# All later adaLN weight panels on VectorE, and one TensorE sum ahead of TensorE's third panel

## The chip, the core and the metric

The kernel runs on one core of one Trainium2 chip. The metric is the device time of one execution in microseconds. A core has TensorE (matrix products, PE in the profile; PEld are its weight loads), VectorE (DVE), ScalarE (ACT), GpSimd (POOL) and SyncE (SP, which here only issues transfers). Each engine runs its own queue in order; they wait for each other on semaphores.

## The reference, cut to what matters

The first of two blocks begins with an adaLN modulation: one vector `c` of 1024 is multiplied by a matrix of 1024 x 6144, and the six parts scale and shift what follows.

```python
mod = jax.nn.silu(c) @ w_ada[i] + b_ada[i]
shift_m, scale_m, gate_m, shift_f, scale_f, gate_f = jnp.split(mod, 6, axis=-1)

h = modulate(rms_norm(x, g_pre_mix[i]), shift_m, scale_m)
p = h @ w_in[i]
...
x = x + gate_m[:, None, :] * rms_norm(merged @ w_out[i], g_post_mix[i])
h = modulate(rms_norm(x, g_pre_ffn[i]), shift_f, scale_f)
...
x = x + gate_f[:, None, :] * rms_norm(f, g_post_ffn[i])
```

Only `shift_m` and `scale_m` (the first third of `mod`) are needed before the projection `h @ w_in`. The other two thirds are used later in the block. The sequence has 256 tokens.

## The kernel before, in words

**adaLN panels.** The matrix `w_ada` is cut into 24 panels of 128 x 2048 f32 (1 MB), each giving two columns of 128 of `mod`. Panels 0 to 7 are needed at once, before the projection. Panels 8 to 23 (the "later" ones, j = 0 to 15) are worked off between the panels of the projection. There are two ways to do a panel:

- On TensorE whole (`pe_ada_whole`, L824): 16 matmuls with the weights stationary and a moving operand of one column.
- On VectorE (`dve_ada`, L790 to L797): ten instructions multiply and add the panel's eight slices into a 128 x 256 sum in `sq_post`; then TensorE sums it over the partitions with two matmuls (`pe_ada`, L804). There are two such sums (`slot`), so VectorE's panel waits on `ada_done` until TensorE has summed VectorE's panel before last.

`ADA_TENSOR` names the panels that TensorE does whole: 1, 3, 5 and, of the later ones, 10, 14, 18 and 22. `ADA_ORDER` is the order in which TensorE comes to the panels: it sets the order of the first eight in its queue, and with `ada_summed` the value of `ada_done` for which others wait.

**Projection.** `h @ w_in` in this stage is 19 panels (`IN1_EARLY`) of 128 x 2048, each for 256 tokens. Weights are f32 and split into a high and a low part: when panel i is done on TensorE, ScalarE makes `w_hi` of panel i + 2 (L660, it reads `land`), then copies panel i's result out (L1373); VectorE makes `w_lo` of panel i + 2 (L667); TensorE then runs 48 matmuls on the panel (L696 to L698). There are two buffers. GpSimd takes each of the first ten results and does the token shift in three instructions (L1614 to L1619).

**Order on VectorE.** After `w_lo` of panel i + 2, VectorE does later adaLN panel j if `ADA_AFTER[j]` is i and the panel is VectorE's. `ADA_AFTER` is 0 to 7, 9 to 15 and 17, so that no adaLN panel stands behind i = 8, 16 and 18.

**Order on TensorE.** TensorE's part of later panel j stands behind projection panel `ADA_AFTER[j] + 2`, or + 1 for one that it does whole.

**SyncE.** It loads `w_in` panel by panel (waits for `lo_ready`), and ahead of some of them the adaLN panel j + 3, once the slot of panel j is free: for a panel of VectorE when its products are done, for one of TensorE when `ada_done` says so. All engines meet at the end of the stage (`stage_end`).

Of the kernel before, what the change touches and what calls it, by code (L numbers as in the profile page):

```python
# [53 lines left out]
ADA_FIRST, ADA_MORE = 8, 3  # L54
# [4 lines left out]
ADA_LATER = 24 - ADA_FIRST  # L59
# [2 lines left out]
IN1_EARLY = IN1 - IN1_ATT - IN1_LATE  # L62
ADA_AFTER = [i * (IN1_EARLY - 2) // (ADA_LATER - 1) for i in range(ADA_LATER)]
assert len(set(ADA_AFTER)) == ADA_LATER
ADA_TENSOR = (1, 3, 5) + tuple(ADA_FIRST + j for j in range(2, ADA_LATER, 4))
ADA_ORDER = (1, 0, 3, 2, 5, 4, 6, 7) + tuple(range(ADA_FIRST, 24))
ADA_VECTOR = tuple(sorted(set(ADA_ORDER) - set(ADA_TENSOR)))
ADA_VECTOR_FIRST = tuple(n for n in ADA_VECTOR if n < ADA_FIRST)
SINGLES, IN2 = 3, 19
# [514 lines left out]
def ada_summed(n):  # L584

    return ADA_ORDER.index(n) + 3

# [5 lines left out]
def load_with_ada(k, sp, d):  # L593

    for i in range(2, IN1):
        if i - 6 in ADA_AFTER:
            j = ADA_AFTER.index(i - 6)
            if j + ADA_MORE < ADA_LATER:
                n = ADA_FIRST + j
                if n in ADA_TENSOR:  # L600
                    sp.wait_ge(k.ada_done, ada_summed(n))
# [145 lines left out]
def pe_project(k, pe, start, count, tiles, W, loop=0, ready=None):  # L747

    n = W.stop - W.start

    def one(i, p, _):
        panel_begin(k, pe, p)
        for o in range(tiles):
            for t in range(KT):
                last = tile_mm(k, k.acc[:, 2 * p.par + o, 0:n], p.par, o * KT + t, k.h_hi[:, t, W],
                               k.h_lo[:, t, W], t == 0, t == KT - 1)
        last.then_inc(k.panel_done, 1)
    peeled = 0  # L760
    if ready is not None:
        p = Panel.of(start, loop)
        panel_begin(k, pe, p)
        for t in range(KT):
            pe.wait_ge(ready[0], ready[1] + (t + 1))
            for o in range(tiles):
                last = tile_mm(k, k.acc[:, 2 * p.par + o, 0:n], p.par, o * KT + t, k.h_hi[:, t, W],
                               k.h_lo[:, t, W], t == 0, t == KT - 1)
        last.then_inc(k.panel_done, 1)
        peeled = 1  # L770
    section(pe, start + peeled, count - peeled, one, loop)
# [45 lines left out]
def pe_ada_whole(k, pe, n):  # L817

    src = k.ada_first[:, n, :] if n < ADA_FIRST else ada_slot(k, n - ADA_FIRST)
    w = src.rearrange("p (o t c) -> p o t c", o=2, t=KT)  # L820
    ada_wait(k, pe, n)
    for o in range(2):
        for t in range(KT):
            last = k.nc.tensor.matmul(k.mb[:, 2, n * 2 + o:n * 2 + o + 1], w[:, o, t], k.csil_mean[:, t:t + 1],  # L824
                                      start=t == 0, stop=t == KT - 1)
    last.then_inc(k.ada_done, 1)
# [21 lines left out]
def pe_project_with_ada(k, pe):  # L848

    def column(n):  # L850
        if n in ADA_TENSOR:
            pe_ada_whole(k, pe, n)
        else:
            pe_ada(k, pe, n)
    pe_project(k, pe, 0, 1, 2, W1, ready=(k.hl_ready, 0))
    done = 0
    for i in range(1, IN1_EARLY):
        pe_project(k, pe, i, 1, 2, W1)
        while done < ADA_LATER and ADA_AFTER[done] + 2 - (ADA_FIRST + done in ADA_TENSOR) <= i:
            column(ADA_FIRST + done)  # L860
# [2057 lines left out]
def program_tensor(k, pe):  # L2918
# [6 lines left out]
    pe.wait_ge(k.csig, 2)  # L2925
    for n in ADA_ORDER[:ADA_FIRST]:
        if n in ADA_TENSOR:
            pe_ada_whole(k, pe, n)
# [300 lines left out]
```

## Time and profile before

| | |
|---|---|
| median of 3 runs | 2144.09 us (2142.82 to 2150.68) |
| the profiled execution's own time | 2144.94 us |
| its span | 2142.9 us |
| TensorE busy | 1988.7 us (93%) |
| VectorE busy | 1404.7 us (66%) |
| mean granted TensorE clock | 0.945 of full speed |

The span is from the first to the last instruction of the profiled execution; its own time is some 2 us more. The stage which the change touches is the first: it ends 197 us into the span. What stands behind it begins when all engines have met. A busy share over the whole span says little on a stage of 197 us, so the rows below are of that stage. A row of the timeline gives the start, the duration, the engine and line, what is written and read, and in brackets how long the engine had been idle and what released it.

### The profile page before, as it was taken

Reading aid. Unit: us, or ns where it says so; the run is one execution under the profiler, and the core shown is the slowest. Engines: PE = TensorE matmul, PEld = TensorE weight load, DVE = VectorE, ACT = ScalarE, POOL = GpSimd, SP = SyncE. Lnnn points to the kernel's source line nnn. Section 1 sums busy time; section 2 is a strip of 40 time slices with the busy share of each in tenths; the row PEclk is TensorE's granted clock in tenths of the full one; section 3 lists DMA queues with packets and bytes.
Section 4 is the critical chain, followed back from the end, with each engine's and each line's share of the span. In section 5 each row is a group of like instructions: output and inputs, shape, how many; then the busy total and the mean of one; then the engine's idle time right before and its main releaser. Section 6 shows DMA issues by size and latency. Waiting matters only on the chain.

```text
span 2142.9 us, 37023 instructions
## 1 busy us (share of the span) xinstructions
PE 1988.7 (93%) x14932; PEld 1909.4 (89%) x14932; DVE 1404.7 (66%) x2184; ACT 898.7 (42%) x1328; POOL 128.5 (6%) x182
## 2 busy tenths in 40 slices
PE   7898798996799999999999899999999999889997
PEld 6897688984699999998889889999999878889997
DVE  6865576765756557755755767756775565667774
ACT  3223254332455444443445454444444354444442
POOL 0520022200000000001100000000000200000000
PEclk7998798987899999999999999999999999999999
DMA  8565110002445535553323435543554322354552
GB/s 339 216 259 180 40 60 1 2 1 61 158 157 176 209 126 172 172 192 109 112 79 121 136 136 173 180 182 133 172 181 172 120 97 99 99 177 141 193 194 101
DMA packets 43447, 301.40 MB, mean 141 GB/s; under 512 B 4736, under 2 KB 6928, under 8 KB 11072
## 3 DMA queue, kind: packets, MB, share of 16 engines
q1 hardware_dynamic: 42736, 296.90, 39.8%
q0 software_dynamic: 592, 2.87, 0.4%
q8 instruction: 81, 1.33, 0.3%
q14 instruction: 38, 0.31, 0.0%
HBM read 298.70 MB, written 1.05 MB: 140 GB/s over the span
## 4 chain that ended last, share of the span: by engine, by line
PE 78%; DVE 10%; DVEq 4%; ACT 3%; issue 2%; DMA 2%; POOL 0%; ACTq 0%; POOLq 0%; SPq 0%
PE acc L696 20%; PE acc L698 20%; PE acc L697 20%; DVE w_lo L667 2%; ACT w_hi L660 2%; PE mb L824 2%; PE acc L2559 2%; PE mb L719 1%; PE mb L1967 1%; PE acc L1967 1%; DVEq L1403 1%; PE mb L2531 1%; DMA land<-in_w_out 1%; PE mb L1964 1%; DVE gla_sq L2897 1%
## 5 line engine op out<-in xcount | busy, mean ns | idle before, releaser
L696 PE MATMUL acc<-h_hi,w_hi 128*128 128x272 f32 (+1 forms) x2960 | 875.6, 296 | 45.4 <-DVE w_lo L667 19.5
L697 PE MATMUL acc<-h_lo,w_hi 128*128 128x272 f32 (+1 forms) x2960 | 858.2, 290 | 0.0
L698 PE MATMUL acc<-h_hi,w_lo 128*128 128x272 f32 (+1 forms) x2960 | 856.3, 289 | 0.0
L667 DVE TENSOR_TENSOR w_lo<-land,w_hi 128x2048 fp32r<-128x2048 f32 (+2 forms) x251 | 576.9, 2299 | 203.0 <-ACT w_hi L660 202.7
L660 ACT ACTIVATE w_hi<-land 128x2048 fp32r<-128x2048 f32 (+2 forms) x251 | 481.8, 1920 | 523.0 <-PE acc L698 461.6
L696 PEld LDWEIGHTS acc<-h_hi,w_hi 128*128 128x128 f32 x2960 | 571.8, 193 | 59.1 <-DVE w_lo L667 21.7
L697 PEld LDWEIGHTS acc<-h_lo,w_hi 128*128 128x128 f32 x2960 | 573.2, 194 | 2.0 <-issue 0.2
L698 PEld LDWEIGHTS acc<-h_hi,w_lo 128*128 128x128 f32 x2960 | 573.9, 194 | 0.0
L696 PE MATMUL acc<-a_hi,w_hi 128*128 128x272 f32 (+1 forms) x880 | 252.3, 287 | 0.6 <-DVE w_lo L667 0.3
L698 PE MATMUL acc<-a_hi,w_lo 128*128 128x272 f32 (+1 forms) x880 | 252.4, 287 | 0.0
L697 PE MATMUL acc<-a_lo,w_hi 128*128 128x272 f32 (+1 forms) x880 | 251.4, 286 | 0.0
L696 PEld LDWEIGHTS acc<-a_hi,w_hi 128*128 128x128 f32 x880 | 166.1, 189 | 1.3 <-DVE w_lo L667 0.9
L697 PEld LDWEIGHTS acc<-a_lo,w_hi 128*128 128x128 f32 x880 | 165.9, 188 | 0.0
L698 PEld LDWEIGHTS acc<-a_hi,w_lo 128*128 128x128 f32 x880 | 165.5, 188 | 0.0
L1094 ACT ACTIVATE sq_post<-acc 128x272 f32<-128x272 f32 (+1 forms) x48 | 18.0, 392 | 184.4 <-PE acc L698 184.4
L1250 DVE TENSOR_TENSOR t_ff<-acc,ssum 128x272 f32<-128x272 f32 (+1 forms) x88 | 38.5, 437 | 83.5 <-PE acc L698 81.1
L696 PE MATMUL acc<-y_hi,w_hi 128*128 128x256 f32 (+1 forms) x192 | 57.3, 298 | 17.8 <-DVEq L546 13.6
L1119 DVE TENSOR_SCALAR f<-acc,vec 128x272 f32<-128x272 f32 (+1 forms) x40 | 19.9, 497 | 74.5 <-ACT sq_post L1094 73.9
L2468 POOL MEMSET sel<- 40x1024 f32 x2 | 1.9, 942 | 1045.8 <-PE acc L707 1045.8
L2336 DVE TENSOR_TENSOR p<-acc,ssum 128x272 f32<-128x272 f32 (+1 forms) x56 | 24.2, 432 | 49.3 <-PE acc L698 48.9
L696 PEld LDWEIGHTS acc<-y_hi,w_hi 128*128 128x128 f32 x192 | 37.2, 194 | 21.3 <-issue 19.2
L697 PE MATMUL acc<-y_lo,w_hi 128*128 128x256 f32 (+1 forms) x192 | 55.3, 288 | 0.0
(519 smaller groups left out, 2589.7 us busy)
## 6 DMA issues: line engine op xcount, KB each, us to landing
land<-in_w_gu SPq DMA_DIRECT2D x110, 1024.0 KB, 4.9
land<-in_w_in SPq DMA_DIRECT2D x65, 1024.0 KB, 4.9
land<-in_w_down SPq DMA_DIRECT2D x40, 1408.0 KB, 6.0
ada_first<-in_w_ada SPq DMA_DIRECT2D x24, 1024.0 KB, 8.6
land<-in_w_ab SPq DMA_DIRECT2D x24, 512.0 KB, 3.5
land<-in_w_out SPq DMA_DIRECT2D x12, 1024.0 KB, 4.9
land<-in_w_in_single SPq DMA_DIRECT2D x6, 512.0 KB, 3.5
const<-in_const POOLq DMA_DIRECT2D x1, 1134.0 KB, 7.9
```

Source lines behind the costliest of these rows:

```text
L660: k.nc.scalar.activation(k.w_hi[:, p.par, 0:size * P], k.land[:, p.par, 0:size * P], ACT.Copy).then_inc(k.hi_ready, 1)
L667: k.nc.vector.tensor_tensor(k.w_lo[:, p.par, 0:size * P], k.land[:, p.par, 0:size * P], k.w_hi[:, p.par, 0:size * P].bitcast(F32), ALU.sub ...
L696: mm(out, k.w_hi[:, par, c], hi, start=start, stop=False)
L697: mm(out, k.w_hi[:, par, c], lo, start=False, stop=False)
L698: return mm(out, k.w_lo[:, par, c], hi, start=False, stop=stop)
L719: r = k.nc.tensor.matmul(k.mb[:, 2, 0:n], k.mean_ones[:, :], moving, start=done == 0, stop=done == KT)
L824: last = k.nc.tensor.matmul(k.mb[:, 2, n * 2 + o:n * 2 + o + 1], w[:, o, t], k.csil_mean[:, t:t + 1], start=t == 0, stop=t == KT - 1)
L1250: v.tensor_tensor(k.t_ff[:, t % 2, W], k.acc[:, 2 * p.par, 0:n], c, ALU.mult).then_inc(k.t1_ready, 1)
L1403: dve.drain()
L1967: last = mm(bank[:, 1, c * P + lo:c * P + hi], m["x_bd"][:, c, :], m["xr"][:, c, lo:hi], start=True, stop=True)
L2336: k.nc.vector.tensor_tensor(chunk_tile(k, l, c), k.acc[:, 2 + o, 0:W.stop - W.start], k.scale[:, W], ALU.mult).then_inc((k.chunk_free, k.a ...
L2559: last = mm(k.acc[:, 0, lo:hi], k.fvz[0:chi - clo, i % 2, c, h, :], k.fpt[0:chi - clo, h, c, 0:n], start=(h == 0 and c == 0), stop=(h == 1 ...
```

## The change

Panels 10, 14, 18 and 22 leave `ADA_TENSOR`, so VectorE does all sixteen later panels. In `ADA_ORDER` panels 4 and 5 change places. SyncE's order stays; four of its waits turn from `ada_done` to `ada_products`.

```diff
-ADA_TENSOR = (1, 3, 5) + tuple(ADA_FIRST + j for j in range(2, ADA_LATER, 4))
-ADA_ORDER = (1, 0, 3, 2, 5, 4, 6, 7) + tuple(range(ADA_FIRST, 24))
+ADA_TENSOR = (1, 3, 5)
+ADA_ORDER = (1, 0, 3, 2, 4, 5, 6, 7) + tuple(range(ADA_FIRST, 24))
```

On TensorE, ahead of the projection (`mb` holds the sums, `sq_post` is what VectorE made, `ada_first` the panels as they landed):

```order
 L804 MATMUL mb<-mean_ones,sq_post 128x1 [waits ada_products]
 L804 MATMUL mb<-mean_ones,sq_post 128x1
+L804 MATMUL mb<-mean_ones,sq_post 128x1 [waits ada_products]
+L804 MATMUL mb<-mean_ones,sq_post 128x1
 L824 MATMUL mb<-csil_mean,ada_first 128x1 [waits ada_first_landed5]
 L824 MATMUL mb<-csil_mean,ada_first 128x1 x15
```

The first pair is the sum of panel 2; the pair with + is the sum of panel 4, which stood behind panel 5's sixteen matmuls and now stands ahead of them.

On TensorE behind projection panel 3, before:

```order
L804 MATMUL mb<-mean_ones,sq_post 128x1 [waits ada_products]
L804 MATMUL mb<-mean_ones,sq_post 128x1
L824 MATMUL mb<-csil_mean,ada_first 128x1 [waits ada_first_landed10]
L824 MATMUL mb<-csil_mean,ada_first 128x1 x15
L696 MATMUL acc<-h_hi,w_hi 128x256 [waits acc_free,lo_ready]
```

The same place with the change:

```order
L804 MATMUL mb<-mean_ones,sq_post 128x1 [waits ada_products]
L804 MATMUL mb<-mean_ones,sq_post 128x1
L696 MATMUL acc<-h_hi,w_hi 128x256 [waits acc_free,lo_ready]
L697 MATMUL acc<-h_lo,w_hi 128x256
L698 MATMUL acc<-h_hi,w_lo 128x256
```

Panel 10's sixteen matmuls are gone from between the two projection panels; a pair like the first stands behind the next projection panel instead. It is so at three more places.

On VectorE, between `w_lo` of projection panel 4 and of panel 5:

```order
-L667 TENSOR_TENSOR w_lo<-land,w_hi 128x2048 [waits hi_ready] x2
+L667 TENSOR_TENSOR w_lo<-land,w_hi 128x2048 [waits hi_ready]
+L790 TENSOR_SCALAR sq_post<-ada_first,csil 128x256 [waits ada_done,ada_first_landed10]
+L790 TENSOR_SCALAR sq_post<-ada_first,csil 128x256
+L790 TENSOR_SCALAR upd<-ada_first,csil 128x256 x2
+L792 SCALAR_TENSOR_TENSOR sq_post<-ada_first,csil,sq_post 128x256 x2
+L792 SCALAR_TENSOR_TENSOR upd<-ada_first,csil,upd 128x256 x2
+L795 TENSOR_TENSOR sq_post<-sq_post,upd 128x2x256
+L797 TENSOR_TENSOR sq_post<-sq_post 128x256
+L667 TENSOR_TENSOR w_lo<-land,w_hi 128x2048 [waits hi_ready]
```

Two splits that stood one behind the other now have panel 10's ten instructions between them. It is so at three more places, and nothing else moves on VectorE.

## Rows read from the trace of the kernel before

**Rows 1.** The page: busy time, share of the span and instructions of each engine.
```profile
PE 1988.7 (93%) x14932; PEld 1909.4 (89%) x14932; DVE 1404.7 (66%) x2184; ACT 898.7 (42%) x1328; POOL 128.5 (6%) x182
```

**Rows 2.** By stretch: length; PE, PEld, DVE, ACT, POOL busy; clock, DMA share, GB/s.
```profile
50.77:133.38 82.61, 76.40 (x593) 75.82 (x592) 69.54 (x80) 24.43 (x21) 44.05 (x30) 0.92 0.63 239
133.38:196.24 62.86, 57.50 (x435) 57.12 (x433) 39.92 (x61) 19.18 (x16) 0.00 (x0) 0.88 0.60 218
```

**Rows 3.** Waits between 50.77 and 196.3: total, times, longest.
```profile
DVE w_lo L667 <- ACT w_hi L660: 33.5, 10, 10.6
```

**Rows 4.** Timeline of VectorE ahead of the projection.
```profile
29.59 0.42 DVE L797 TENSOR_TENSOR sq_post<-sq_post 128x256 f32<-128x256 f32 x1
...
32.68 0.61 DVE L790 TENSOR_SCALAR sq_post<-ada_first,csil 128x256 f32<-128x256 f32 x2 [2.66 <-PE mb L804]
...
36.75 2.28 DVE L667 TENSOR_TENSOR w_lo<-land,w_hi 128x2048 fp32r<-128x2048 f32 x1
```

**Rows 5.** Timeline of TensorE ahead of the projection.
```profile
23.90 0.99 PE L804 MATMUL mb<-mean_ones,sq_post 128*128 128x1 f32 x4
24.75 6.96 PE L824 MATMUL mb<-csil_mean,ada_first 128*128 128x1 f32 x32
31.58 1.84 PE L804 MATMUL mb<-mean_ones,sq_post 128*128 128x1 f32 x8
```

**Rows 6.** Timeline of VectorE in the projection, splits and one first adaLN instruction.
```profile
50.77 2.29 DVE L667 TENSOR_TENSOR w_lo<-land,w_hi 128x2048 fp32r<-128x2048 f32 x1 [2.15 <-ACT w_hi L660]
...
61.94 2.28 DVE L667 TENSOR_TENSOR w_lo<-land,w_hi 128x2048 fp32r<-128x2048 f32 x1
64.38 1.15 DVE L790 TENSOR_SCALAR sq_post<-ada_first,csil 128x256 f32<-128x256 f32 x2 [0.16 <-issue]
...
70.53 2.29 DVE L667 TENSOR_TENSOR w_lo<-land,w_hi 128x2048 fp32r<-128x2048 f32 x1
...
133.38 2.28 DVE L667 TENSOR_TENSOR w_lo<-land,w_hi 128x2048 fp32r<-128x2048 f32 x1
...
139.91 2.28 DVE L667 TENSOR_TENSOR w_lo<-land,w_hi 128x2048 fp32r<-128x2048 f32 x1
...
187.43 2.29 DVE L667 TENSOR_TENSOR w_lo<-land,w_hi 128x2048 fp32r<-128x2048 f32 x1 [10.56 <-ACT w_hi L660]
...
193.96 2.28 DVE L667 TENSOR_TENSOR w_lo<-land,w_hi 128x2048 fp32r<-128x2048 f32 x1
```

**Rows 7.** Timeline of GpSimd, the token shift of one projection panel.
```profile
63.14 1.98 POOL L1614 TENSOR_TENSOR c<-p_in 128x512 f32 x1 [1.41 <-ACTq L1375]
65.35 1.08 POOL L1617 TENSOR_TENSOR c<-c,vec 128x512 f32<-128x512 f32 x1 [0.23 <-issue]
66.58 1.30 POOL L1619 TENSOR_TENSOR p_in<-p_in,c 128x512 f32 x1 [0.15 <-issue]
```

**Rows 8.** Timeline of TensorE: a wait for `w_lo`, and two whole panels.
```profile
64.27 0.39 PE L696 MATMUL acc<-h_hi,w_hi 128*128 128x256 f32 x1 [1.59 <-DVE w_lo L667]
...
71.94 3.71 PE L824 MATMUL mb<-csil_mean,ada_first 128*128 128x1 f32 x32
...
141.88 5.04 PE L824 MATMUL mb<-csil_mean,ada_first 128*128 128x1 f32 x32
```

**Rows 9.** TensorE by stretch: stretch, length, busy (x), granted clock, DMA share, GB/s.
```profile
65.40:68.80 3.40, 3.40 (x19) 0.52 0.87 342
146.80:150.70 3.90, 3.90 (x19) 0.50 1.01 391
```

**Rows 10.** Timeline of ScalarE: splits, each released by the end of a projection panel.
```profile
60.37 1.91 ACT L660 ACTIVATE w_hi<-land 128x2048 fp32r<-128x2048 f32 x1 [3.31 <-PE acc L698]
...
154.57 1.92 ACT L660 ACTIVATE w_hi<-land 128x2048 fp32r<-128x2048 f32 x1 [10.46 <-PE acc L698]
...
160.28 1.92 ACT L660 ACTIVATE w_hi<-land 128x2048 fp32r<-128x2048 f32 x1 [3.31 <-PE acc L698]
...
166.43 1.92 ACT L660 ACTIVATE w_hi<-land 128x2048 fp32r<-128x2048 f32 x1 [3.74 <-PE acc L698]
```

## The prediction

> **What bounds the kernel now.** I read the page first: TensorE is busy 93% of the 2142.9 us span [rows 1]. That says little here, because the change touches only the first 197 us, and behind them all engines meet, so whatever the stage gains or loses is passed on whole. So I read the stage by stretches, its waits, and then the queues of the four engines.
>
> In the stretch of the first ten projection panels (50.77 to 133.38) VectorE is busy 69.5 of 82.6 us and TensorE 76.4; in the other nine 39.9 and 57.5 of 62.9 [rows 2]. Neither engine is the bound alone. The loop between them is: TensorE finishes panel i, ScalarE makes `w_hi` of i + 2 (1.92 us), VectorE makes `w_lo` (2.29 us), and TensorE may begin i + 2. A projection panel at full clock takes TensorE 160.28 - 154.57 = 5.71 us, and 6.15 with one pair of L804 behind it (166.43 - 160.28) [rows 10]. A round of VectorE, one `w_lo` and one adaLN panel, takes 139.91 - 133.38 = 6.53 us when GpSimd is quiet, 2.28 of it the split and 4.25 the panel; beside one token shift of GpSimd it takes 70.53 - 61.94 = 8.59, and 61.94 - 50.77 = 11.17 beside two [rows 6]. So where VectorE has an adaLN panel to do it is slower than TensorE, and TensorE waits: panel 3's first matmul starts at 64.27, right behind its `w_lo`, and panel 2 had ended at 60.37 [rows 8, 10]. Where TensorE does the panel whole it is the other way round: 3.7 us at full clock, 5.04 for panel 18 [rows 8], and behind each the granted clock is down for a while: 0.50 of full speed, that is 1.2 GHz, over 146.80 to 150.70 [rows 9]. Meanwhile VectorE waits for `w_hi`: 33.5 us in ten waits, the longest 10.56 us, in front of `w_lo` at 187.43 [rows 3, 6]. The stage is thus a sum: VectorE's work, plus its waits behind TensorE's slow places. The end of the stage is VectorE's too: `w_lo` at 187.43, one adaLN panel, and `w_lo` from 193.96 to 196.24 [rows 6].
>
> **The change part by part.**
>
> *The order of the first eight.* VectorE's panel 7 uses the slot of panel 4 and waits until TensorE has summed it. Panel 4's products are there before 24, but its sum stands behind whole panel 5 (24.75 to 31.7), and VectorE sits idle 2.66 us until 32.68 [rows 4, 5]. With the sum in front, TensorE does it at about 24.9, and panel 7 starts as soon as panel 6 is finished, at 30.01, plus a gap of 0.3 (estimate between the 0.16 of [rows 6] and the 0.6 that I allow for draining): a gain of 2.66 - 0.3 = 2.3 us, with 2.0 and 2.5 as ends. What is late next: TensorE's panel 5 ends one pair later (a pair is recorded as four matmuls, the row of 0.99 us; two pairs took 1.84, so 0.9 each [rows 5]), at about 32.6; the sum of 6 follows at 33.5, that of 7 at about 35.4. VectorE reads them only behind its `w_lo` at 36.75 + 2.28 = 39.03, which becomes 36.7 [rows 4], so they are 1.3 us early. The first projection panel and all behind it start 2.3 us earlier.
>
> *Four whole panels leave TensorE, four go to VectorE.* On VectorE forty instructions are added: 4 x 4.25 = 17.0 us [rows 6]. On TensorE 4 x 3.7 to 5.0 us go, with the slow clock behind each, and four pairs (0.44 each) come. Now count VectorE's time from the start of `w_lo` of panel 2 to the end of the last: 196.24 - 50.77 = 145.5 us. Of the 33.5 us of waits 2.15 lie before its start, so 31.3 lie in it, and 114.1 are work. With the change the work is 114.1 + 17.0 = 131.1, plus what GpSimd takes.
>
> *GpSimd.* Its ten token shifts slow VectorE only while an adaLN panel is worked on: the split takes 2.28 to 2.29 us with GpSimd or without [rows 6], but the first two of the ten instructions take 1.15 beside a shift and 0.61 without [rows 4, 6]. One shift is 1.98, 1.08 and 1.30 us [rows 7] and costs the round 8.59 - 6.53 = 2.06; two cost 11.17 - 6.53 = 4.64. Over the twelve rounds of before, seven have such a surcharge (8.6 to 8.7 five times, 11.0 and 11.2 once each), together 19.7 us; the shift of panel 8 met no adaLN panel. With the change all of the first nine rounds have one, and all ten shifts can meet it: 20.6 to 23.2 at 2.06 to 2.32 each, so 0.9 to 3.5 more. I take 2.3, one more shift at the dearer price.
>
> *Waits that stay.* With VectorE at 8.6 us a round and TensorE at 6.15, TensorE has its panel done long before `w_hi` is wanted. From the end of `w_lo` i to the start of `w_lo` i + 2 VectorE has two adaLN panels and one split, 2 x 4.25 + 2.28 = 10.8 us when GpSimd is quiet; TensorE and ScalarE need 6.15 + 1.95 = 8.1. So no wait while each round has an adaLN panel. Only where one is left out the slack goes: behind i = 16, VectorE has 4.25 + 2.28 = 6.5 against 8.1, a wait of 1.6. Behind i = 8 GpSimd's surcharge still covers it. I take 2.0 in all, with 1.3 and 5 as ends.
>
> *TensorE's sums.* Each pair waits on products made in the same round; the projection panel behind it needs a `w_lo` that comes on VectorE behind those products anyway, so the pair (0.44) is hidden in the 2.28 of the split. VectorE's wait on `ada_done` for the panel before last is met when projection panel i is done, which `w_lo` i + 2 has already waited for.
>
> *SyncE.* The adaLN slot is now freed by VectorE's products in all cases. SyncE's queue is in order, and the `w_in` load behind it waits for a `lo_ready` that is later on VectorE than those products, so nothing is held up. Two megabytes per round of 6.53 us are some 320 GB/s; the stretch 146.80 to 150.70 moved 391 [rows 9], and a load has more than a round to land. Taken as nothing; if it were not hidden a landing would be late by a microsecond or two in the last nine panels, which is in the upper bound.
>
> *Sum.* 2.3 + 31.3 - 17.0 - 2.3 - 2.0 = 12.3 us. The profiled execution took 2144.9 us (0.8 above the median of the runs), so 2144.9 - 12.3 = 2132.6 us. The last `w_lo` would end at about 184 instead of 196.2.
>
> **A rule against it.** A row first: beside the shift of 63.14 to 67.88, whose instructions last 4.4 us, the round from 61.94 lost 2.06 us, since one VectorE instruction waits behind each GpSimd instruction and the next slips in between [rows 6, 7]. By that row ten shifts cost VectorE 20.6 us. The Trainium skill, in "SBUF — State Buffer", section "SBUF: two separate sides", says that VectorE (with two SBUF inputs or a two-port mode) and GpSimd share one port pair as a lock, and that the loser is blocked for the other's whole instruction. Read as if VectorE lost the shift's whole 4.4 us each time, the sum would be 44 us in place of 22, and the change 22 - 12.3 = 9.7 us slower than before; the rows show half of that or less per shift, so I go by them; it is the second half of rival D.
>
> **Rivals.**
>
> *A. VectorE alone sets the pace* (the sum above): 2132.6, its own range 2129 to 2136. Chance 0.64.
>
> *B. TensorE's clock follows the idle time.* In the first ten rounds TensorE will idle some 8.6 - 6.15 = 2.5 us in each. The 3.9 us before 64.27 were followed by a clock of 0.52 over 65.40 to 68.80 [rows 8 to 10]. At half clock a panel takes 11.4 us instead of 5.7. If that lasts a whole panel, TensorE and ScalarE need 11.8 + 1.95 = 13.8 against VectorE's 2 x 6.3 + 2.28 = 14.9 in the first ten rounds (hidden) but against 10.8 in the last nine: 3 us each time. Two such, or before's run having been hit worse by its two slow stretches behind panels 18 and 22 than most are, give 4 to 7 us of the gain back: 2138. For it: the clock did fall behind waits. Against: in the last nine rounds TensorE idles only 0.4 us in 6.5. Chance 0.22.
>
> *C. More than the sum*, because the shifts fall partly beside splits: 2128. Chance 0.06.
>
> *D. Slower: GpSimd takes more from VectorE.* If each of the first nine rounds took 11.17, like the one at 50.77, and not 8.6, VectorE would pay 9 x 4.64 = 41.8 us instead of 22: 19.8 more, 2152. It decides from 34.3 us of surcharge on, 3.8 for each of the nine. Against: those two dear rounds each met two shifts, and there are ten shifts in all. So does the second half: if every shift cost VectorE its whole length of 4.4 us, ten would cost 44, 22 more, 2154.6; the 2.06 us of the round from 61.94 speak against it [rows 6, 7]. Chance 0.03 for the first half, 0.01 for the second.
>
> *E. Nothing comes of it:* VectorE's added 19.3 us eat the waits and the order of the first eight is covered by something that the rows don't show, such as a late landing of panel 7: 2143. Chance 0.04.
>
> **How the numbers follow.** Half a per cent (10.7 us), about what a measurement of this kernel can tell from no change, lies at 2133.4. A gives faster in seven of eight of its cases, and C always: 0.56 + 0.06 = 0.62. The rest of A, B and E are within it, 0.34; D is slower, 0.04. The range of eight in ten leaves out D, E and a little at either end: 2127.5 to 2140.
>
> **What the profile after would show.** VectorE's first adaLN instruction of panel 7 at about 30.3 with no wait for L804; no L824 row behind 33; waits of `w_lo` on `w_hi` under 5 us in sum between panels 2 and 20, against 31.3; nine rounds of about 8.6, then of 6.53; the last `w_lo` ending near 184; TensorE waiting for `w_lo` some 2 us before most panels. A granted clock near 0.5 in the last nine rounds would speak for B; rounds of 11 us for D.

## The result, and the profile after

| | us |
|---|---|
| before, median of 9 runs | 2143.2 (2140.33 to 2150.68) |
| changed, median of 9 runs | 2132.67 (2119.26 to 2144.54) |
| ratio, 95% interval | 0.9942 (0.9914 to 0.9969) |
| the profiled execution of the changed kernel: own time, span | 2144.54, 2141.5 |

The changed kernel is faster by 0.6%, 2132.67 us where 2132.6 was forecast. That the two agree to 0.1 us is luck: the interval of the ratio alone is 5.9 us wide to either side. Its profiled execution is the slowest of the nine, so its span says little by itself. The stage has to be read apart from what stands behind it.

The same kinds of rows as before the change ([rows 3] and [rows 2]), now from the changed kernel. The waits between 50.2 and 188.4 us (total, times, longest):

```profile
ACT w_hi L660 <- DMA land<-in_w_in: 17.0, 4, 5.7
...
DVE w_lo L667 <- ACT w_hi L660: 6.5, 3, 3.1
```

VectorE's waits for `w_hi` went from 33.5 us in ten [rows 3] to 6.5 in three, and TensorE now waits for `w_lo` nine times, 11.0 us in all, where it was three times and 4.0. The first row is new: four times ScalarE waits for a landing and not for TensorE.

The busy times by stretch, the first ten rounds and the last nine panels (length; PE, PEld, DVE, ACT, POOL busy; clock, DMA share, GB/s):

```profile
50.20:134.96 84.76, 69.49 (x513) 68.06 (x513) 80.40 (x100) 23.97 (x21) 39.29 (x30) 0.90 0.61 232
134.96:188.37 53.41, 47.66 (x400) 47.20 (x398) 47.55 (x80) 19.63 (x17) 0.00 (x0) 0.99 0.71 256
```

In the first stretch VectorE is busy 80.4 of 84.8 us, where it was 69.5 of 82.6: the stretch is 2.2 us longer than it was [rows 2]. The second is 9.4 us shorter, and its granted clock is 0.99 where it was 0.88 [rows 2]. So the gain lies in the second.

VectorE's timeline of the changed kernel, ahead of the projection, in the first rounds, and in the last:

```profile
31.80 0.61 DVE L790 TENSOR_SCALAR sq_post<-ada_first,csil 128x256 f32<-128x256 f32 x2 [0.17 <-issue]
...
50.20 2.29 DVE L667 TENSOR_TENSOR w_lo<-land,w_hi 128x2048 fp32r<-128x2048 f32 x1 [2.46 <-ACT w_hi L660]
...
61.35 2.28 DVE L667 TENSOR_TENSOR w_lo<-land,w_hi 128x2048 fp32r<-128x2048 f32 x1
...
69.96 2.29 DVE L667 TENSOR_TENSOR w_lo<-land,w_hi 128x2048 fp32r<-128x2048 f32 x1
...
79.09 2.29 DVE L667 TENSOR_TENSOR w_lo<-land,w_hi 128x2048 fp32r<-128x2048 f32 x1
...
148.02 2.29 DVE L667 TENSOR_TENSOR w_lo<-land,w_hi 128x2048 fp32r<-128x2048 f32 x1
...
154.54 2.29 DVE L667 TENSOR_TENSOR w_lo<-land,w_hi 128x2048 fp32r<-128x2048 f32 x1
...
179.55 2.29 DVE L667 TENSOR_TENSOR w_lo<-land,w_hi 128x2048 fp32r<-128x2048 f32 x1 [3.15 <-ACT w_hi L660]
...
186.08 2.29 DVE L667 TENSOR_TENSOR w_lo<-land,w_hi 128x2048 fp32r<-128x2048 f32 x1
```

Panel 7 starts 0.17 us behind panel 6, no longer 2.66 [rows 4]. The rounds take 11.15, 8.61 and 9.13 us while GpSimd works and 6.52 later. In front of `w_lo` of panel 19 there are 3.15 us of wait instead of 10.56 [rows 6]. The last `w_lo` ends at 188.4, before at 196.2: the stage is 7.9 us shorter. The span is only 1.4 us shorter, so 6.5 us were lost behind the stage in this execution.

### The profile page after: what moved, and what is told of

Read it like the earlier page. It is cut to its first block, busy times and chain, and to the rows that moved or that the text cites. A ratio compares the mean times of both kernels' runs of the same rounds, so it can differ in the third digit from the quotient of the medians.

```text
span 2141.5 us, 36859 instructions
## 1 busy us (share of the span) xinstructions
PE 1980.5 (92%) x14820; PEld 1899.4 (89%) x14820; DVE 1426.0 (67%) x2224; ACT 898.8 (42%) x1328; POOL 125.2 (6%) x182
## 4 chain that ended last, share of the span: by engine, by line
PE 73%; DVE 14%; DVEq 5%; ACT 3%; DMA 2%; issue 2%; POOL 0%; ACTq 0%; SPq 0%; POOLq 0%
PE acc L696 19%; PE acc L698 18%; PE acc L697 18%; DVE w_lo L667 3%; ACT w_hi L660 2%; PE acc L2559 2%; DVEq L843 1%; PE mb L719 1%; PE acc L1967 1%; PE mb L1967 1%; DVEq L1403 1%; DMA land<-in_w_in 1%; PE mb L2531 1%; DVE upd L792 1%; DMA land<-in_w_out 1%
## 5 line engine op out<-in xcount | busy, mean ns | idle before, releaser
L698 PE MATMUL acc<-y_hi,w_lo 128*128 128x256 f32 (+1 forms) x192 | 55.2, 287 | 0.0
```

The costliest lines, as they stand in the source:

```text
L698: return mm(out, k.w_lo[:, par, c], hi, start=False, stop=stop)
```

## The experiments

Each experiment is compared with runs of the kernel before on the same chip, and these had medians of 2145.2 to 2148.3 us on the three chips used. So compare the ratios, not the medians. "Last `w_lo`" is the end of the last split of this stage in the run's one profiled execution; "behind it" is that execution's span less this. "Short shift" and "cheaper shift" are the changed kernel with less work on GpSimd.

| kernel | median us (runs) | ratio to before, interval | last `w_lo` | behind it |
|---|---|---|---|---|
| before (first profile) | 2143.2 (9) | | 196.2 | 1946.7 |
| before again | 2148.77 (10) | 1.0013 (0.9997 to 1.0029) | 195.7 | 1941.2 |
| changed (first profile) | 2132.67 (9) | 0.9942 (0.9914 to 0.9969) | 188.4 | 1953.1 |
| changed again | 2134.35 (12) | 0.9951 (0.9932 to 0.9971) | 185.1 | 1938.1 |
| order of the first eight only | 2144.89 (12) | 0.9999 (0.9984 to 1.0014) | 193.9 | 1951.0 |
| panels to VectorE only | 2132.67 (6) | 0.9938 (0.992 to 0.9957) | 189.8 | 1941.4 |
| loads moved and held | 2143.14 (12) | 0.9988 (0.9974 to 1.0003) | 191.7 | 1949.7 |
| two loads later | 2136.76 (11) | 0.9949 (0.9932 to 0.9967) | 184.9 | 1937.9 |
| TensorE keeps 10 and 14 | 2133.97 (8) | 0.9948 (0.993 to 0.9965) | 184.2 | 1946.8 |
| TensorE keeps 18 and 22 | 2147.12 (12) | 0.9998 (0.9982 to 1.0014) | 197.2 | 1949.8 |
| short shift | 2117.78 (4) | 0.9862 (0.983 to 0.9894) | 164.0 | 1954.2 |
| cheaper shift | 2120.89 (6) | 0.9886 (0.9866 to 0.9906) | 172.7 | 1946.7 |

**One half of the change at a time.** The order of the first eight alone:

```diff
-ADA_ORDER = (1, 0, 3, 2, 5, 4, 6, 7) + tuple(range(ADA_FIRST, 24))
+ADA_ORDER = (1, 0, 3, 2, 4, 5, 6, 7) + tuple(range(ADA_FIRST, 24))
```

> The order of the first eight alone, the later panels as before. Theory A (the stage is VectorE's work plus its waits, and most of the gain is in the waits behind TensorE's whole panels): VectorE's wait of 2.7 us in front of panel 7 goes, but the first projection panels gain less, 0.5 to 2 us, since w_in panel 2 lands only at about 48 us; in all 0 to 2 us under before. Theory B (the order of the first eight carries the gain, because everything behind it starts earlier): 8 to 12 us under before.

And the later panels alone:

```diff
-ADA_TENSOR = (1, 3, 5) + tuple(ADA_FIRST + j for j in range(2, ADA_LATER, 4))
+ADA_TENSOR = (1, 3, 5)
```

> The later panels all on VectorE, the order of the first eight as before. Theory A: 8 to 10 us under before, the waits of w_lo on w_hi between 50 and 190 us under 8 us in sum instead of 31, and the wait of 2.7 us in front of panel 7 still there. Theory B: within 3 us of before.

Theory B falls: the order alone gives no difference that can be measured (0.9999, and its interval allows some 3 us either way), the panels alone give the whole gain (0.9938). With the panels alone the wait in front of panel 7 is there, and longer: TensorE's granted clock was 0.50 over 16 to 19 us in this execution, and in the first profile of the kernel before it was still 1.00 up to 17. VectorE's timeline:

```profile
35.22 0.61 DVE L790 TENSOR_SCALAR sq_post<-ada_first,csil 128x256 f32<-128x256 f32 x2 [3.52 <-PE mb L804]
```

The order-only kernel ends the stage at 193.9, against 196.2 and 195.7, but this isn't the order's effect alone: at the start of `w_lo` of panel 2 it is ahead by 0.7 and 1.1 us only (50.03 against 50.77 and 51.08). What the order is worth at equal clock is read from several profiles further down.

**The changed kernel once more.**

> The changed kernel once more, on the same chip as the others: the profiled execution was the slowest of nine (2144.5 us against a median of 2132.7). If that was TensorE's clock behind the stage, this one has its last w_lo ending at 184 to 189 us as before it, and a time nearer 2132; the difference to the other execution lies behind 200 us and goes with the time at half clock. If the stage itself varies, the end of the stage lies elsewhere by as much as the times do.

The last `w_lo` ends at 185.1 and the time is 2125.1 us, 19.4 under the other execution of the same kernel. Only 3.3 of it are in the stage; 15 are behind it, and the last 1.1 outside the span. Of the 15, 14.2 arise in the next stage, the attention. TensorE from the last `w_lo` to one and the same VectorE instruction there (L2151), in the first profile and then in this one (length, PE busy, clock, DMA share, GB/s):

```profile
188.40:366.70 178.30, 150.96 (x930) 0.83 0.13 44
```

```profile
185.10:349.20 164.10, 138.69 (x930) 0.92 0.15 48
```

The work is the same, 930 matmuls; the granted clock is 0.83 in the one and 0.92 in the other. A mean of 0.83 is 34% of 178 us at 1.2 GHz, 0.92 is 16% of 164: some 34 us less at half speed, which is up to 17 us of TensorE's work where TensorE is the bound. So the table's last column varies by 16 us (1937.9 to 1954.2) in no order of what the kernels do, and the stage has to be compared by its own end. What in the phase of work and clock decides it wasn't settled.

**In which half of the stage the gain lies.**

```diff
-ADA_TENSOR = (1, 3, 5)
+ADA_TENSOR = (1, 3, 5, 10, 14)
```

> The changed kernel, but TensorE keeps panels 10 and 14 whole (both in the stretch where GpSimd shifts); VectorE has 18 and 22. Theory A (a whole panel costs TensorE and its clock what an added round costs VectorE while GpSimd works, so the gain lies in the last nine projection panels): within 3 us of the changed kernel, 2131 to 2137. Rival C (the gain lies in the first ten panels, where TensorE's waits are shortened): 5 us or more slower than the changed kernel.

```diff
-ADA_TENSOR = (1, 3, 5)
+ADA_TENSOR = (1, 3, 5, 18, 22)
```

> The changed kernel, but TensorE keeps panels 18 and 22 whole (where GpSimd is quiet); VectorE has 10 and 14. Theory A: 6 to 10 us slower than the changed kernel, 2140 to 2144, with a wait of some 10 us of w_lo of panel 19 on w_hi and a granted clock of 0.5 behind both whole panels. Rival C: within 3 us of the changed kernel.

The first is as fast as the changed kernel (0.9948), the second as slow as the kernel before (0.9998). Its 2147.12 us lie above the 2140 to 2144 that were expected, but the kernel before took 2148.3 on this chip; the distance to the changed kernel is some 10 us by the ratios, as expected. So giving panels 10 and 14 to VectorE brings nothing, and the whole gain comes from 18 and 22.

The stage itself says more than the medians: the first two panels cost something. From the start of `w_lo` of panel 2 to the end of the last it takes 134.4 us with 10 and 14 left on TensorE, where the changed kernel takes 138.2 and 136.6; and 148.9 with 18 and 22 left there, where the kernel before takes 145.5 and 144.6. The stretches tell why. In the first, five waits of `w_lo` on `w_hi` of the kernel before (10.4 us in sum) shrink to one of 0.88, but 8.5 us of adaLN work come, and VectorE's surcharge from GpSimd grows by 3.1: 2.2 us lost. In the second, waits of 21.0 us shrink to 3.15 for the same 8.5 us of work: 9.4 gained.

VectorE's timeline with 18 and 22 on TensorE shows the two waits that then come back:

```profile
157.44 2.29 DVE L667 TENSOR_TENSOR w_lo<-land,w_hi 128x2048 fp32r<-128x2048 f32 x1 [6.25 <-ACT w_hi L660]
...
188.38 2.29 DVE L667 TENSOR_TENSOR w_lo<-land,w_hi 128x2048 fp32r<-128x2048 f32 x1 [10.59 <-ACT w_hi L660]
```

**GpSimd's share.** The token shift on 8 columns of 256; the rest of the shift is left out, so the output isn't the reference's:

```diff
-        g.tensor_tensor(k.c1[:, 0:2, :], k.p_in[:, two, 0:SEQ], k.p_in[:, two, 1:SEQ + 1], ALU.subtract)
+        g.tensor_tensor(k.c1[:, 0:2, 0:8], k.p_in[:, two, 0:8], k.p_in[:, two, 1:9], ALU.subtract)
...
```

> The changed kernel with GpSimd's token shift on 8 of 256 columns only (the rest of the shift is left out). If the surcharge of the shifts is 20 to 24 us and VectorE sets the pace: every round with an adaLN panel takes 6.5 to 6.7 us, the last w_lo ends 18 to 23 us earlier, 2110 to 2118 in all. If TensorE's clock or the landings set the pace as soon as VectorE is faster: rounds of 7 to 8 us, and the gain stays under 12 us.

VectorE's timeline of its first rounds:

```profile
49.60 2.29 DVE L667 TENSOR_TENSOR w_lo<-land,w_hi 128x2048 fp32r<-128x2048 f32 x1 [2.14 <-ACT w_hi L660]
...
56.13 2.28 DVE L667 TENSOR_TENSOR w_lo<-land,w_hi 128x2048 fp32r<-128x2048 f32 x1
```

Every round with an adaLN panel is 6.5 us now. From the start of `w_lo` of panel 2 to the end of the last it takes 164.0 - 49.6 = 114.4 us, against 138.2 and 136.6 in the two profiles of the changed kernel. Waits aside, VectorE is busy 105.1 us of it, against 127.9 in both of these profiles: GpSimd costs VectorE 22.8 us, and nothing else took its place.

**Loads.** Since ScalarE waited for landings, adaLN panels 9 and 10 go behind `w_in` panel 2, and each later adaLN load is held until the `w_in` load ahead of it has landed:

```diff
+                q = Panel.of(i - 1)
+                sp.wait_ge(k.landed[q.par], q.landed())
...
         load(k, sp, p.par, p.half, flat(d["w_in"], i), IN_K)
+        if i == 2:
+            for n in (ADA_FIRST + 1, ADA_FIRST + 2):
+                sp.dma_start(k.ada_first[:, n, :], flat(d["w_ada"], n)).then_inc(k.ada_first_landed[n], 16)
```

> The changed kernel, with adaLN panels 9 and 10 loaded behind w_in panel 2, and each later adaLN load held until the w_in load ahead of it has landed. If late landings of w_in take part of the gain (w_hi waited for landings four times in the last nine panels and once at 48 us): those waits shrink from 17 us to under 6, w_in panel 2 is there at about 44 us, the wait in front of w_lo of panel 19 falls from 3.2 to about 1.6, the stage ends 2 to 4 us earlier than in the changed kernel. If the landings are late for want of bandwidth and not for their order, nothing moves.

A miss. SyncE's queue is in order: the held adaLN load also held the `w_in` load behind it, so that two went out together. SyncE's timeline in that kernel:

```profile
158.75 0.33 SPq L606 DMA_DIRECT2D ada_first<-in_w_ada  x1
159.12 0.43 SPq L573 DMA_DIRECT2D land<-in_w_in  x1
```

`w_lo` of panel 19 waits 5.17 us for `w_hi` in it. In the changed kernel the same `w_in` load leaves at 156.86. ScalarE's waits for landings grew from 17.0 us in four to 36.1 in eight, and the last `w_lo` came 3.3 us later than in the slower of the two profiles of the changed kernel. Without the hold:

> The changed kernel with adaLN panels 9 and 10 loaded behind w_in panel 2 and nothing held. In the run that also held the later loads, w_in panel 2 was no longer waited for, but the hold delayed the loads of w_in behind it. If that is the whole story: w_hi of panel 2 is released by TensorE and not by a landing, the waits in the last nine panels are those of the changed kernel, 0 to 2 us under the changed kernel. If the two loads are missed by what waits for them: a wait on ada_first in front of panel 9 or 10, or on w_in panel 3, and up to 4 us over.

0.9949, the same as the changed kernel. No wait on a landing is left on ScalarE from panel 2 on, and the last `w_lo` ends at 184.9 against 188.4 and 185.1. By the wait in front of panel 19, 3.15 us in the first profile and 1.55 here, the landings were worth 1.6 us there; in the second profile of the changed kernel, which also waited for landings, that wait was 1.54 already.

**A version that beats both.** The shift is spread so that GpSimd has one instruction for a panel:

```diff
+        for u in range(2):
+            a(shift_part(k, i)[:, u, 1:SEQ + 1], k.acc[:, 2 * p.par + u, 0:SEQ], ACT.Copy, scale=vec(k, "mu", 2 * i + u))
+            last = a(k.p_in[:, 2 * i + u, 1:SEQ + 1], k.acc[:, 2 * p.par + u, 0:SEQ], ACT.Copy,
+                     scale=k.keep[:, 2 * i + u:2 * i + u + 1])
...
+        g.tensor_tensor(k.p_in[:, two, 1:SEQ + 1], k.p_in[:, two, 1:SEQ + 1], shift_part(k, i)[:, :, 0:SEQ],
+                        ALU.add).then_inc(k.shifted, 1)
```

`keep` is 1 - mu, made once on VectorE; `shift_part` is one of two buffers in `c1`.

> The changed kernel with a cheaper shift: ScalarE, while it copies a result out, writes mu times it and (1 - mu) times it (four instructions in place of one), and GpSimd is left with one addition per panel in place of three instructions. If VectorE loses time behind each GpSimd instruction (22 to 24 us for thirty, by the kernel with the short shift): ten are left, the surcharge falls to 7 to 10 us, the last w_lo ends some 13 to 16 us earlier, at 170 to 174 us, 2118 to 2124 in all. If ScalarE's longer copy delays w_hi instead: rounds stay above 8 us and the time within 5 us of the changed kernel.

0.9886 (0.9866 to 0.9906), 24.8 us under the kernel before and, by the ratios, about 14 under the changed one. VectorE's timeline shows one round, with one slow instruction, and its length of 7.57 us (its lines are two further down):

```profile
72.82 2.29 DVE L669 TENSOR_TENSOR w_lo<-land,w_hi 128x2048 fp32r<-128x2048 f32 x1
...
77.29 1.92 DVE L794 SCALAR_TENSOR_TENSOR upd<-ada_first,csil,upd 128x256 f32<-128x256 f32 x2
...
80.39 2.29 DVE L669 TENSOR_TENSOR w_lo<-land,w_hi 128x2048 fp32r<-128x2048 f32 x1
```

The pair at 77.29 takes 1.92 where it takes 0.88 alone. From `w_lo` of panel 2 to the end it is 123.0 us, 8.7 over the short shift. VectorE is busy 114.7 of it, 9.7 more than with the short shift, and waits 1.1 less: ten GpSimd instructions cost it 0.97 each.

**The kernel before once more.**

> The kernel before once more, for a second profile: the stage's rounds fall at other places of TensorE's clock. If the terms read from one profile hold: the last w_lo ends at 193 to 198 us, waits of w_lo on w_hi between panels 2 and 20 of 28 to 33 us in sum, and the wait of 2.7 us or more in front of panel 7 is there. If the one profile was a lucky or unlucky one: it ends outside of that.

The last `w_lo` ends at 195.7 us, and there is a wait of 2.38 in front of panel 7, a little under the 2.7 that was expected; 33.1 us of waits in ten, of which 30.5 lie behind the start of `w_lo` of panel 2. So the profile that the forecast was read from was a usual one in the stage.

## Why the prediction was right, by its own steps

*What bounds the stage* was right: VectorE's work plus its waits. The time it gave, 135.4 us from the start of `w_lo` of panel 2 to the end of the last (114.1 + 17.0 + 2.3 + 2.0), was 138.2 and 136.6. The work was 134.1 in both, where 133.4 was forecast; the rest is waits. The stage was to end 12.3 us earlier, at 184; it ended 7.9 earlier in the first profile and 11 in the second. The gain of the medians, 10.5 us, is nearer to the second. The forecast time came out to 0.1 us because it was counted down from one execution of the kernel before, 1.7 us above the median of the nine, and the sum was about as much too large.

*The order of the first eight*, forecast at 2.3: the wait in front of panel 7 went as told, 0.17 us are left of it, and panel 7 starts at 31.80 in the first profile and 30.13 in the second, where 30.3 was forecast. At the start of `w_lo` of panel 2 the gain is 0.6 us in the first profile (50.20 against 50.77 [rows 6]) and 2.2 in the second (48.58). TensorE's timeline tells why the first is short; the first whole panel of the changed kernel, in the first and in the second profile:

```profile
14.03 4.80 PE L824 MATMUL mb<-csil_mean,ada_first 128*128 128x1 f32 x32
```

```profile
13.54 3.63 PE L824 MATMUL mb<-csil_mean,ada_first 128*128 128x1 f32 x32
```

The granted clock fell inside the first of them (1.00 up to 16.0 us, 0.50 from 17.0 on), so all sums came later, and VectorE waited 1.86 us in front of panel 6 instead of 0.60. Both cases occur with both orders, so like can be compared with like at the start of `w_lo` of panel 0. Where the first whole panel took 3.63 us, it starts at 34.20, 34.37 and 34.38 with the new order (changed again, two loads later, TensorE keeps 18 and 22), and at 36.75 and 36.64 with the old. Where it took 4.8 to 5.1, it starts at 35.88 and 36.41 with the new (changed, order only), and at 39.29 with the old (panels only). Four more with the new order lie between, 4.1 to 4.3 us and 35.6 to 36.0. The term was right in size, 2.3 to 2.6 us at equal clock and some 3 in the worse case, but it is a term of 0.1%, and the times of the run with the order alone can't tell it from nothing.

*Four panels to VectorE*, 17.0, and *the waits of 31.3 that go*: right, the waits left are 4.0 us (0.88 and 3.15) in the first profile and 2.4 in the second, where 2.0 were forecast. The 0.88 stands in front of panel 12 in both, behind the pair of splits of i = 8, where the prediction had GpSimd's surcharge cover all of the 1.6; it covered 0.7 (with the short shift the wait at this place is 1.54). The excess of the first profile is the step on *SyncE*, taken as nothing: ScalarE waited for landings, which is the microsecond or two that the prediction named as its bound.

*GpSimd*, forecast at 22.0 us in all: 22.8 by the short shift, 2.3 for each of the ten token shifts, inside the 2.06 to 2.32 that were read from two rounds; single rounds paid 2.6 (9.13 - 6.53). One reading under it was wrong. The prediction took the split as free of GpSimd, 2.28 to 2.29 us with it or without. It is so in every row of the kernel before, but in the changed kernel the split at 113.33 took 3.27 us; its row is in the last section. It is one reason why VectorE's surcharge is a little larger than forecast.

The Trainium skill, in "SBUF — State Buffer", section "SBUF: two separate sides", says that the loser of the port pair that VectorE and GpSimd share is blocked for the other's whole instruction. The trace agrees for a single instruction, as far as it can show it: a pair of VectorE instructions took 1.04 us more beside a GpSimd instruction of 1.39 us, and the split 0.99 more beside one of 1.18. The runs don't agree with the sum that the second half of rival D made of this, in which VectorE loses all of GpSimd's time: GpSimd's thirty instructions in the changed kernel last 39.3 us in sum (1.0 to 3.1 each), and VectorE lost 0.76 us for each. Part of their length is GpSimd's own waiting for VectorE, as the last section shows. Rivals C and D fell with it.

*Rival B*, the clock: in the first stretch it was 0.90 in both profiles, and the slow panels were hidden behind VectorE's rounds as worked out; in the last nine panels it was 0.99 and 1.00. What the prediction missed is the clock behind the stage. Its range of 2127.5 to 2140 holds the median and six of the nine runs; those at 2119.26, 2124.09 and 2144.54 lie outside, the last being the profiled one.

*What it said of where the gain lies* was only half drawn out. The sum charges four panels alike. The runs show that the two in GpSimd's reach are worth nothing, and cost 2 to 4 us in the stage: on VectorE they take 4.25 us each and a surcharge, and that is more than the waits that go with them. All of the gain is in panels 18 and 22.

## What to carry to other kernels

When two engines feed each other, move work to the one with more idle time only where the receiver's round stays shorter than the giver's; here it was so for two of four panels, and the other two cost 2 to 4 us in the stage. Before counting an engine's idle time as room, ask which other engine lengthens its work: thirty short GpSimd instructions cost VectorE more (22.8 us) than four added panels (17), and taking twenty of them away gained more than the change did. Where executions of one kernel differ by 15 us in stretches that the edit doesn't touch, compare the end of the edited stage, and take the times from many runs. The edited stage has its luck too: compare profiles in which the clock fell at the same place.

## What the runs showed of the hardware

The same kernel's executions spread over 25 us (2119.26 to 2144.54) with the granted clock's mean going from 0.957 to 0.945; over the nine runs time and clock go together (correlation -0.93).

A split of VectorE and a GpSimd instruction don't run side by side in the rows that follow: whichever starts second waits. In the kernel with the short shift GpSimd's instructions on 16 elements take 0.3 us, but 2.2 where one starts inside a `w_lo` (GpSimd's timeline):

```profile
56.30 2.18 POOL L1614 TENSOR_TENSOR c<-p_in 128x16 f32 x1 [3.03 <-ACTq L1375]
```

The split of 56.13 ends at 58.41 and the GpSimd instruction at 58.48; the split itself takes its 2.28 us. The other way round, in the first profile of the changed kernel, the GpSimd instruction is first by 0.05 us, and `w_lo` of panel 9 takes 3.27 us (GpSimd's timeline and VectorE's):

```profile
113.28 1.18 POOL L1619 TENSOR_TENSOR p_in<-p_in,c 128x512 f32 x1 [0.15 <-issue]
...
113.33 3.27 DVE L667 TENSOR_TENSOR w_lo<-land,w_hi 128x2048 fp32r<-128x2048 f32 x1
```

A GpSimd instruction that starts inside a split isn't free for VectorE either. In the kernel with the cheaper shift the one of 57.31 lasts 3.05 us, past the end of the split, and the first adaLN pair behind it takes 1.39 us instead of 0.61.
